# Wide feature units, one-matmul channel sums and a shift through device memory in a three-layer forward pass

## What is computed

```python
# first block
h = rms_norm(x, norm1_g);  a, gate, q, k, v = split(h @ w_in)      # 5 x 512 columns
y = depthwise_conv31(a * sigmoid(gate)) + dw_bias                  # over positions
conv_out = silu(layer_norm(y, conv_ln_g, conv_ln_b))               # over 512 channels
attn_out = neighbourhood_attention(rms(q), rms(k), v, rpb)         # 8 heads of 64
x = x + concat(conv_out, attn_out) @ w_out
h = rms_norm(x, norm2_g);  x = x + (silu(h @ w_gate) * (h @ w_up)) @ w_down
# second block, layers l = 0, 1
u = rmsnorm(x, norm_mix[l])
q, k, v, iq, ik, iw, cB, cC, ch, g = split(u @ w_in_2[l])
y_attn = top_k_attention(q, k, v, iq, ik, iw) @ w_attn_out[l]
y_conv = (cB * short_conv(cC * ch)) @ w_conv_out[l]
x = x + (sigmoid(g0) * y_attn + sigmoid(g1) * y_conv) @ w_mix_out[l]
x = x + square(relu(rmsnorm(x) @ w_mlp_up[l])) @ w_mlp_down[l]
# end
return rmsnorm(x, norm_final)
```

## Time and profile before

| | |
|---|---|
| median of 3 runs | 1049.14 us |
| the three runs | 1047.73, 1049.14, 1053.33 us |
| profiled execution, its own time | 1050.84 us |
| its span in the trace | 1049.0 us |
| TensorE busy | 1030.5 us (98%) |
| VectorE, ScalarE, GpSimd busy | 707.7, 535.9, 69.6 us |
| mean granted clock of TensorE | 0.993 |

### The profile page before, as it was taken

One profiled execution on the slowest core, in us unless ns is written; L12 is line 12 of the kernel. 1 busy time (PEld: TensorE's weight loads), 2 busy tenths in 40 slices (PEclk: granted clock), 3 DMA queues, 4 the chain that ended last, 5 costly groups with the idle time before them and its releaser, 6 DMA issues.

```text
span 1049.0 us, 16345 instructions
## 1 busy us (share of the span) xinstructions
PE 1030.5 (98%) x6205; PEld 895.4 (85%) x6205; DVE 707.7 (67%) x1073; ACT 535.9 (51%) x687; POOL 69.6 (7%) x80
## 2 busy tenths in 40 slices
PE   8989999999999999999999999999999999999997
PEld 7865788888888899998888888888999988888886
DVE  6876776666667686768666656667776677655655
ACT  6545575444457534455645444475344646444443
POOL 1000000000000309000000000011170000000000
PEclk9989999999999999999999999999999999999999
DMA  9975345555556653248465563665632674565521
GB/s 295 218 223 176 104 139 199 201 170 195 180 185 186 201 176 121 80 164 294 147 223 179 189 211 105 226 202 163 198 101 81 221 241 165 196 206 195 170 90 41
DMA packets 130653, 185.13 MB, mean 176 GB/s; under 512 B 4361, under 2 KB 106399, under 8 KB 130591
## 3 DMA queue, kind: packets, MB, share of 16 engines
q1 hardware_dynamic: 130503, 184.25, 54.4%
q10 hardware_dynamic: 88, 0.04, 0.0%
HBM read 180.91 MB, written 1.56 MB: 174 GB/s over the span
## 4 chain that ended last, share of the span: by engine, by line
PE 93%; DVE 2%; ACT 1%; DMA 1%; SPq 1%; issue 1%; DVEq 0%; ACTq 0%
PE wide L561 19%; PE wide L568 10%; PE acc L524 9%; PE acc L525 9%; PE acc L526 9%; PE wide L524 7%; PE wide L525 7%; PE wide L526 7%; PE wide L544 3%; PE wide L537 3%; PE wide L538 3%; SPq L438 1%; PE acc L704 1%; PE acc L738 1%; DMA big<-cu 1%; PE acc L725 1%
## 5 line engine op out<-in xcount | busy, mean ns | idle before, releaser
L1294 DVE TENSOR_TENSOR wlo<-raw,whi 128x2048 fp32r<-128x2048 f32 (+1 forms) x178 | 387.1, 2181 | 156.7 <-ACT whi L980 155.6
L980 ACT ACTIVATE whi<-raw 128x2048 fp32r<-128x2048 f32 (+1 forms) x178 | 322.1, 1819 | 105.5 <-PE wide L526 43.9
L561 PE MATMUL wide<-uhl,whi 128*128 128x512 f32 x864 | 207.3, 391 | 0.0
L561 PEld LDWEIGHTS wide<-uhl,whi 128*128 128x128 f32 x864 | 160.7, 188 | 33.7 <-DVE uhl L1319 1.2
L524 PE MATMUL acc<-whi,mhi 128*128 128x512 f32 x376 | 147.8, 393 | 0.3 <-DVE mlo L1372 0.3
L524 PE MATMUL wide<-uhl,whi 128*128 128x256 f32 x512 | 147.0, 287 | 1.0 <-DVE wlo L1379 0.9
L525 PE MATMUL acc<-wlo,mhi 128*128 128x512 f32 x376 | 146.9, 391 | 0.0
L526 PE MATMUL acc<-whi,mlo 128*128 128x512 f32 x376 | 146.5, 390 | 0.0
L525 PE MATMUL wide<-uhl,whi 128*128 128x256 f32 x512 | 144.9, 283 | 0.0
L526 PE MATMUL wide<-uhl,wlo 128*128 128x256 f32 x512 | 144.9, 283 | 0.0
L568 PEld LDWEIGHTS wide<-uhl,wlo 128*128 128x128 f32 x864 | 110.8, 191 | 4.2
(11 more groups left out here) (248 smaller groups left out, 1218.6 us busy)
## 6 DMA issues: line engine op xcount, KB each, us to landing
raw<-in_w_in SPq DMA_DIRECT2D x49, 1024.0 KB, 5.3
raw<-in_w_mlp_up SPq DMA_DIRECT2D x32, 1024.0 KB, 5.5
raw<-in_w_mlp_down SPq DMA_DIRECT2D x32, 1024.0 KB, 4.9
raw<-in_w_gate SPq DMA_DIRECT2D x11, 1024.0 KB, 5.3
raw<-in_w_up SPq DMA_DIRECT2D x11, 1024.0 KB, 5.4
raw<-in_w_down SPq DMA_DIRECT2D x11, 1024.0 KB, 5.5
raw<-in_w_mix_out SPq DMA_DIRECT2D x8, 1024.0 KB, 6.6
raw<-in_w_out SPq DMA_DIRECT2D x4, 1024.0 KB, 10.5
```

Of the source, the lines that this page charges most:

```text
L561: pe.matmul(col[2 * n + c][:], whi_v(u)[:, f, c * P:c * P + P], uhl[:, f, :], start=f == 0, stop=False)
L980: act.activation(whi[:, u.buf, 0:size], raw[:, u.slot, 0:size], ACT.Copy).then_inc(w_hi, 1)
L1294: dve.tensor_tensor(wlo[:, u.buf, 0:size], raw[:, u.slot, 0:size], whi[:, u.buf, 0:size].bitcast(F32), ALU.subtract).then_inc(w_lo, 1)
```

## The change

- The 14 feature units of each layer are computed by `wide_features` into `wide[0]` and `wide[1]` in turn. ACT copies the second halves into the destination, DVE adds the first halves and then multiplies by `rnb`. A unit now waits for the evacuation of the unit two places back. The banks of the next eight units are renumbered, and `feature_evac` moves ahead of the split and of the softmax's normalization.
- The shift goes through device memory: one store of half of `cu`, then 8 loads. The skewed copy and the bias loads move behind it.
- The channel sums are one matmul each. POOL adds the chunks of `y`, DVE adds those of the squares.
- The first token tile's rows of unit 10 are multiplied at p = 2, around the turning of head 6. Orders on ACT and DVE move with it, and the reciprocal is made in two halves.
- At the end, squares are summed by quarters, POOL multiplies the left half of each tile by the gain, ACT scales it, DVE makes the right half, and four stores take the place of two.

SyncE's queue, first block:

```diff
+            def shift_store(half):
+                sp.wait_ge(glu, half + 1)
+                if half:
+                    sp.wait_ge(bias_in, 16 * 2)
+                sp.dma_start(scratch[half], cu[:, 2 * half:2 * half + 2, :]).then_inc(shift_out, 16)
             def shift(half):
-                sp.wait_ge(glu, half + 1)
+                sp.wait_ge(shift_out, 16 * (half + 1))
                 if half:
                     sp.wait_ge(conv_ps, 2)
                 for s in range(SHIFTS):
-                    for q in range(SHIFTS):
-                        into = shifted[SHIFT_CH * s:SHIFT_CH * s + SHIFT_CH, :, :].rearrange("p (c q) x -> p c q x", q=SHIFTS)
-                        sp.dma_start(into[:, :, q, :], cu[SHIFT_CH * q:SHIFT_CH * q + SHIFT_CH, 2 * half:2 * half + 2, s:s + SHIFTED])\
+                    for c in range(2):
+                        src = bass.AP(tensor=d["skew"].tensor, offset=scratch[half].offset + c * half_cu + s,
+                                      ap=[[rows_cu, SHIFT_CH], [SHIFT_CH * rows_cu, SHIFTS], [1, SHIFTED]])
+                        sp.dma_start(shifted[SHIFT_CH * s:SHIFT_CH * s + SHIFT_CH, SHIFTS * c:SHIFTS * c + SHIFTS, :], src)\
                             .then_inc(shift_in, 16)
...
                 if j == 8:
-                    shift(0)
-                if j == 3:
+                    shift_store(0)
...
                     sp.dma_start(skewed, runs).then_inc(skew_in, 16)
-                if j == 5:
+                if j == 9:
+                    shift(0)
                     sp.wait_ge(skew_in, 16)
...
                 load(a_unit(A_OUT + i), w_out[:, 2 * r:2 * r + 2, :])
+                if i == 0:
+                    shift_store(1)
                 if i == 1:
                     shift(1)
```

TensorE, first block and layers:

```diff
                 if p < 2:
                     convolve(2 + p)
+                    turn_probs(0, 2 * p)
                 elif p == 2:
-                    pe.wait_ge(conv_sb, KA)
-                    for c in range(KA):
-                        mm = pe.matmul(MU[:, 0:T], ones[:], y[:, c, :], start=c == 0, stop=c == KA - 1)
-                    mm.then_inc(ln_mu, 1)
-                else:
-                    pe.wait_ge(ln_sq, 2)
-                    for c in range(KA):
-                        mm = pe.matmul(VAR[:, 0:T], ones[:], lnsq[:, c, :], start=c == 0, stop=c == KA - 1)
-                    mm.then_inc(ln_var, 1)
-                turn_probs(0, 2 * p)
+                    pe.wait_ge(y_sum, KA - 1)
+                    pe.matmul(MU[:, 0:T], ones[:], ysum, start=True, stop=True).then_inc(ln_mu, 1)
+                    turn_probs(0, 2 * p)
                 turn_probs(0, 2 * p + 1)
+                if p == 2:
+                    pe.wait_ge(w_lo, a_unit(A_OUT).upto())
+                    pe.wait_ge(o_lo, 2)
+                    pe.wait_ge(s_max, HEADS)
+                    first_rows(0, lambda: turn_probs(0, HEADS - 2))
+            pe.wait_ge(sq_sum, 2)
+            pe.matmul(VAR[:, 0:T], ones[:], lnsq[:, 0, :], start=True, stop=True).then_inc(ln_var, 1)
             value_pair(0, HEADS // 2 - 1)
...
-                    if j >= 12:
-                        pe.wait_ge(fevac, A_FEATURES + L_FEAT * l + j - 11)
+                    if j >= 10:
+                        pe.wait_ge(fevac, A_FEATURES + L_FEAT * l + j - 9)
...
-                        col_features(u, col[(j + 2) % 4], uhi, ulo)
+                        wide_features(u, (j + 1) % 2)
```

ScalarE, layers, behind the split of unit j + 2 (in the first block `o_split(0, 1)` now comes first at p = 2, and behind the squares a square root on one column is added):

```diff
+                    elif j >= L_FIRST:
+                        act.wait_ge(used, u.upto())
+                        if j in (8, 10):
+                            act.wait_ge(qk_ps, 4 * (1 + l) + j - 6)
+                        act.activation(feature_dst(j), wide[(j + 1) % 2][:, :, T:2 * T], ACT.Copy).then_inc(flow, 1)
```

VectorE, first block at p = 3, then behind the root, then the layers:

```diff
+                    dve.wait_ge(ln_sq, 2)
+                    dve.tensor_tensor(lnsq[:, 0:2, :], lnsq[:, 0:2, :], lnsq[:, 2:4, :], ALU.add).then_inc(sq_sum, 1)
+                    dve.wait_ge(sq_sum, 1)
+                    dve.tensor_tensor(lnsq[:, 0, :], lnsq[:, 0, :], lnsq[:, 1, :], ALU.add).then_inc(sq_sum, 1)
+                    split(a_unit(A_OUT + 2))
...
-            link(dve.reciprocal(lnr, lnsd))
+            link(dve.reciprocal(lnr[:, 0:P], lnsd[:, 0:P]))
+            o_split(0, 3)
+            link(dve.reciprocal(lnr[:, P:T], lnsd[:, P:T]))
...
-                    dve.tensor_tensor(dst, col[(j + 2) % 4][:].rearrange("p (c t) -> p c t", c=2),
-                                      rnb[:].unsqueeze(1).broadcast_to([P, 2, T]), ALU.mult).then_inc(fevac, 1)
+                    dve.wait_ge(flow, L_FEAT * l + j - L_FIRST + 1)
+                    link(dve.tensor_tensor(dst, wide[(j + 1) % 2][:, :, 0:T], dst, ALU.add))
+                    dve.tensor_tensor(dst, dst, rnb[:].unsqueeze(1).broadcast_to([P, 2, T]), ALU.mult).then_inc(fevac, 1)
...
                     if j >= 14:
                         softmax_max(1 + l, j - 14)
+                    if j > L_FIRST:
+                        feature_evac(j - 1)
+                    if j >= 14:
                         softmax_norm(1 + l, j - 14)
                     if j:
                         split(l_unit(l, j + 2), unit_size(True, j + 2))
-                    if j > L_FIRST:
-                        feature_evac(j - 1)
```

GpSimd, first block:

```diff
+            pool.wait_ge(qk_T, 4)
+            for c in range(1, KA):
+                pool.wait_ge(conv_sb, c + 1)
+                first = y[:, 0, :] if c == 1 else ysum
+                pool.tensor_tensor(ysum, first, y[:, c, :], ALU.add).then_inc(y_sum, 1)
+                pool.wait_ge(y_sum, c)
```

The end, on ScalarE, VectorE, GpSimd and SyncE's queue:

```diff
+            for i, (t, h) in enumerate(QUARTERS):
+                act.wait_ge(x_new, quarter_count(last, i))
+                act.activation(big[:, 2 * i:2 * i + 2, :].rearrange("p a b -> p (a b)"), x[:, t, h * 512:h * 512 + 512], ACT.Square,
+                               accum_out=ss[:, i:i + 1]).then_inc(sq_done, 1)
...
+                act.activation(xnt[:, t, 0:512], xnt[:, t, 0:512], ACT.Copy, scale=rn[:, t:t + 1]).then_inc(fin_act, 1)
...
-                dve.scalar_tensor_tensor(xnt[:, t, :], x[:, t, :], rn[:, t:t + 1], gfin, ALU.mult, ALU.mult).then_inc(fin, 1)
+                dve.scalar_tensor_tensor(xnt[:, t, 512:D], x[:, t, 512:D], rn[:, t:t + 1], gfin[:, 512:D], ALU.mult, ALU.mult)\
+                    .then_inc(fin, 1)
...
+                pool.tensor_tensor(xnt[:, t, 0:512], x[:, t, 0:512], gfin[:, 0:512], ALU.mult).then_inc(xg_ok, 1)
...
-                sp.wait_ge(fin, t + 1)
-                sp.dma_start(d["out"][0, t * P:(t + 1) * P, :], xnt[:, t, :]).then_inc(out_done, 16)
+                for h, ready in ((1, fin), (0, fin_act)):
+                    sp.wait_ge(ready, t + 1)
+                    cs = slice(h * 512, h * 512 + 512)
+                    sp.dma_start(d["out"][0, t * P:(t + 1) * P, cs], xnt[:, t, cs]).then_inc(out_done, 16)
```

More of the change, by code:

```diff
@@ L78 @@
 G_N = G_LAYER + LAYERS * LG_N
-LAYER_LINKS = 91
+LAYER_LINKS = 105
 L_FIRST = 8
@@ L150, in build @@
                      ap=[[GRID_W * SKEW_RUN, HEADS], [SKEW_RUN, GRID_W], [1, SKEW_RUN]])
+    half_cu = T + 2 * PAD + 1
+    rows_cu = 2 * half_cu
+    scratch = [bass.AP(tensor=d["skew"].tensor, offset=at, ap=[[rows_cu, P], [half_cu, 2], [1, half_cu]])
+               for at in (HEADS * GRID_W * SKEW_RUN, 0)]
     w_in2, w_attn2, w_conv2 = per_layer("w_in_2"), per_layer("w_attn_out_2"), per_layer("w_conv_out_2")
@@ L296, in build @@
         conv_sb = sem("conv_sb")
+        y_sum = sem("y_sum")
+        sq_sum = sem("sq_sum")
         ln_mu = sem("ln_mu")
@@ L326, in build @@
         ff_lo = sem("ff_lo")
+        part_ok = sem("part_ok")
+        xg_ok = sem("xg_ok")
         fin = sem("fin")
+        fin_act = sem("fin_act")
         dve_chain = sem("dve_chain")
@@ L399, in first_block, with feature_dst @@
             return isinstance(a, int) and a == 0
+        def feature_dst(j):
+            return (cC, cH, cB)[(j - 8) // 2][:, 2 * (j % 2):2 * (j % 2) + 2, :] if j < 14 else \
+                big[:, 2 * (j - 14):2 * (j - 14) + 2, :]
         def t_bank(a, h):
@@ L803, in _, with first_rows @@
                     turn((qtok, ktok)[n], n)
+            def first_rows(t, between):
+                r = A_OUT_ROWS[0]
+                return rows_half(a_unit(A_OUT), t, mhi[:, 2 * r:2 * r + 2, :], mlo[:, 2 * r:2 * r + 2, :], True, False, between)
             for p in range(HEADS // 2):
@@ L1110, in _ @@
             for p in range(HEADS // 2):
-                for e in range(2):
-                    h = 2 * p + e
-                    if h + 2 < HEADS:
-                        exps(0, h + 2)
-                    copy_probs(0, h)
-                    if e == 0 and p >= 1:
-                        o_split(0, p - 1)
-                for c in range(2 if p == 2 else 0):
-                    f = slice(2 * c, 2 * c + 2)
-                    act.wait_ge(ln_xc, c + 1)
-                    act.activation(lnsq[:, f, :], y[:, f, :], ACT.Square).then_inc(ln_sq, 1)
+                h = 2 * p
```

(26 more changed lines are left out.)

67 lines of the change are left out of this document (31 added, 36 removed).

## The result

| | before | after |
|---|---|---|
| median, in the runs side by side | 1050.08 us (4 runs) | 1037.05 us (4 runs: 1036.79, 1037.01, 1037.10, 1041.51) |
| profiled execution | 1050.84 us | 1037.01 us |
| its span | 1049.0 us | 1035.2 us |
| TensorE, VectorE, ScalarE, GpSimd busy | | 1020.0, 736.7, 552.3, 85.2 us |

The ratio is 0.9883, with a 95% interval of 0.9856 to 0.9910: 13.0 us faster. In the two profiled executions the spans differ by 13.8 us, where the prediction's sum was 18.2. The sign and the range held, the range by 1 us of its slow end (1038); 4.4 us of the sum did not come.

The account below looks back on a forecast made before the run. TensorE, busy for 98% of the span, was taken to bound the kernel. Shift 6.4, norm 5.0, features 6.2 and end 0.6 sum to 18.2 us: 1032.6 from 1050.84, 1030.9 from the median; forecast 1031.5 us, range 1027 to 1038.

Parts of the forecast that it names:

- rival A: The shifted rows are late again, landing at 53 to 56 us, low clock back; 1035 to 1038 us; 15%.
- rival B: The norm's chain keeps its place, TensorE waits for the split convolution half; gain 2 instead of 5, 1034.5 us; 12%.
- The shift, 6.4 us: At the convolution after unit 6: 3.8 us of wait for shifted channels plus 2.63 us of low clock saved.
- so I take 3 MB: landing at 40 to 50.4, at least 1.7 us early: Traffic from 32.9 us on taken as 3 MB, at 171 to 407 GB/s, so the shifted rows land in time.
- The norm, 5.0 us: At the convolution's norm: 6.1 us saved at most, less about 1 us of new waits; bounds 2 and 6.1.
- (a): Channel sum of the norm: four sums took 1.99 us, one takes 0.5, saving 1.5 us.
- (b): Square sums of the norm: 3.11 us at the low clock, one takes 0.5 at full clock, saving 2.6 us.
- (c): TensorE's wait of 2.03 us before a value pair is filled with 2.9 us of rows that came later.
- New waits ... about 1 us: In the norm: head 6's turning waits about 1 us for its normalization; value pair 3 about 0.5; 1.0 us subtracted.
- The features, 6.2 us: Wide units in the layers: 5.56 us instead of 5.79, 28 units x 0.23 = 6.4, taken as 6.2; bounds 0 and 6.4.
- C: VectorE binds the feature units: wide units gain nothing and lose 0.1 us each, 1040.5 us; 6%.
- D: A slot's release stands in series with the softmax on VectorE: 1.8 us per head unit, 1060.5 us; 3%.

Follow-up runs that it names:

- skewed copy early: The changed kernel with the skewed copy back behind unit 3, unit 9's load still ahead of the shift: 1035.75 us (ratio 0.9884).
- two adds: The changed kernel with GpSimd's first add held until two heads have their maxima and the third chunk's add replaced by a second matmul: 1037.46 us.
- shift alone: The kernel before with only the shift through device memory: 1046.05 us (ratio 0.9960).
- changed kernel once more: The changed kernel run and profiled a second time, nothing altered: 1037.64 us.
- features alone: The kernel before with only the wide feature units: 1045.17 us against 1051.51 (ratio 0.9943).

## Why the prediction was right, and what it had wrong

**Right.** Faster, and inside the range, though 5.6 us above the forecast: the slow end was set for rivals A and B together, and a part of each came. The wide units run without a wait for their slots; the two sums have two records each; `convolve(0)` and `convolve(1)` take 3.6 us (53.61 to 57.20); in the profiled execution there is no stretch at 0.50 from the shift to the rows; the end gave 0.6, as was said.

**The shift, 6.4 us.** The sum was right for a shift in time: with the skewed copy early, the way from unit 1 to unit 7 is 44.29 - 37.84 = 6.45 us shorter. It was not in time. The step that failed is "so I take 3 MB: landing at 40 to 50.4, at least 1.7 us early". The rows came at 53.6 and 54.1, so 5.9 us were gained in one profiled execution and 4.2 in the other. The prediction had counted the skewed copy as 0.5 of 4 MB at one rate, like weights; out of the way, this copy alone was enough to have the rows in time. The landing was what rival A feared, its price mostly was not. Over seven traces TensorE waits 0.5 to 2.1 us; in six of them the clock does not fall, in one (two adds) it does, and 3.2 us are lost against the profiled execution. That the rival did not cost more was luck: 2.1 us of wait left the clock up in one execution, 1.9 did not in another.

Beside rival A the prediction set the Trainium skill's page DMA: Bandwidth & Descriptors (section Why small descriptors are slow (HBM only)): small pieces are slow from and to device memory, not between SBUF places. The runs fit a part of it and prove none. The copy in device memory, in small pieces, cost about as much as twice its bytes of weights. But the shift's own pieces, now from device memory, took 6.4 to 11.2 us to land in the traffic, about as long as the 7.9 to 11.7 of those between SBUF places with half the bytes in each load, and 2.6 to 4.3 us out of it.

**The norm, 5.0 us; 3.3 came.** Terms (a), (b) and (c), 6.1 us together, were about right on TensorE. Wrong was "New waits ... about 1 us". They add up to 0.44 (`nmx`) + 0.61 (`mlo`) + 0.27 (`xn`) + 0.47 (`prob`) + 0.6 (`wlo`) = 2.4 us. What is left, about 0.6 us by difference, is in the changes of operands around the pieces that were moved between other work (the next matmul begins 0.31 us later instead of 0.23), which the prediction left out. Of the waits the first two come from GpSimd, which holds VectorE by 0.5 us an add; with two adds 0.9 us came back. The prediction had that case as "at worst 1.7 us" and set it at nothing, since the sum comes late enough; it had asked whether the adds are in time and not what VectorE does meanwhile. And of (b), 1.6 us belonged to the clock, which did not fall in the trace of the shift alone; against that trace the norm's part is worth 64.96 - 63.25 = 1.7 us.

The last wait, for `wlo`, is a small form of rival B: the low part of unit 13 stands on VectorE behind the split of the convolution half, and TensorE has its first six matmuls with that half and then waits:

```profile
114.13 0.39 PE L553 MATMUL acc<-whi,mhi 128*128 128x512 f32 x1
116.23 0.50 PE L553 MATMUL acc<-whi,mhi 128*128 128x512 f32 x1 [0.58 <-DVE wlo L1339]
```

The prediction had read 122.53 as the first such matmul of the kernel before. By the program's order it is the one at 123.21, behind the 24 of unit 11 that begin at 117.77, so the slack was 1.2 us and not 0.5. The sign "some 11.4 us earlier, at 111" failed: it is 9.1 us, at 114.13.

The Trainium skill's page GPSIMD Engine Reference (section 1. Specifications) was cited for the one kind of VectorE instruction that contends with GpSimd, that with two SBUF inputs. The same line names a second kind, instructions in a two-port mode. The rotation with two inputs went from 0.69 to 1.21 us, as the page has it. The normalization with a single tensor went from 0.62 to 1.18; this fits the second kind, but no row shows its mode.

**The features, 6.2 us; 5.2 came.** The step was "5.79 each ... A wide unit takes 5.56". The first is an average over six units that holds the changes of operands at both ends, the second the inside of a run. Like with like, 34.72 us stand against 391.16 - 357.57 = 33.59: 0.19 per unit.

**Rivals C and D.** The prediction was right that neither decides, and wrong about how near they are. D was to decide "from a hold of 2.6 us per unit on". One operation of 0.7 us per unit was enough to make the kernel slower than before. The mechanism was for the greater part not the slot, at which TensorE waited 2.6 of the 11.0 us, but the normalization that the change put behind the evacuation (8.4 us): with 0.9 us of room, and with VectorE's idle time elsewhere. A chance of 3% for D was too low for what the rows allowed one to know.

**The sum.** Of the 4.4 us that are missing in the profiled execution, 0.5 are the shift's, 1.7 the norm's, 1.0 the features', 1.0 the late start and 0.2 a longer wait at the beginning of layer 1 (0.51 for `uhl` and `x` instead of 0.25), which was not followed up.

**The clock's share.** A part of the gain is the clock's, and a single trace does not tell how much. In the 21 executions of the kernel before that ran beside the changed kernel once more, the mean granted clock lies between 0.990 and 0.998 and averages 0.994; the slowest (1055.32 us) had 0.990 and the fastest (1044.67 us) 0.998. The four of the changed kernel average 0.998. By the same rule as above, 0.004 x 1050 gives an estimate of 4 us of the 13.9 between the medians.

**Open.** Why the clock of the first unit rises earlier in some executions than in others, why the skewed copy is so dear (no run changed its pieces), and why a wait of about 2 us was followed by a low clock in three traces (2.03 before and with the features alone, 1.93 with two adds) and not in two (2.03 with the shift alone, 2.13 in the changed kernel once more). With one trace of each kernel it is not shown that the shift alone keeps the clock up at the square sums.

## What to carry to other kernels

Price a wait behind a moved instruction by the order of its engine, not by the slack of the buffer: ask for each consumer of that engine how long before its need it is done, in the stretch where the engine is fullest. An add that is free on GpSimd is paid on VectorE if VectorE is late there; put it where VectorE idles, or leave the work on TensorE. And compare a unit inside a run with another inside a run.

## What was not expected of the hardware

- A copy of 0.5 MB within device memory delayed the transfers beside it by 3 to 5 us, about what 1 MB of weights did (3 to 4.5).
- The same wait of 2.03 us cost 1.6 us more by the clock in one trace than in the other.
- 0.7 us of extra work of VectorE per unit cost 1.15 us per head unit in layer 0 (63.26 instead of 54.07 us for eight): the waits came with a low clock of TensorE.
